# Block stages: three passes over the inner tiles instead of three products per tile

## The chip, the cores and the metric

The kernel runs on one core of a Trainium2 chip. The metric is the device time of one execution in microseconds (us). The engines are TensorE (PE in the profile; PEld is its loading of weights), VectorE (DVE), ScalarE (ACT), GpSimd (POOL) and SyncE (SP), which here only issues DMAs.

## The reference, cut to what matters

A first block (two recurrent branches and a mixture of experts) is followed by a second one with two layers. Each layer of the second block ends in a chain of dense steps, and it is this chain that the change touches:

```python
x = x + g1 * yx                       # yx = o @ w_out, o from attention or from the gated recurrence
hx2 = rms_norm_2(x, norm2_g[layer]) * (1.0 + sc2) + sh2
x = x + g2 * conv_glu(hx2, ffn_w_up[layer], ffn_conv_w[layer], ffn_conv_b[layer], ffn_w_down[layer])

def conv_glu(h, w_up, conv_w, conv_b, w_down):
    gate, val = jnp.split(h @ w_up, 2, axis=-1)
    return (jax.nn.silu(dwconv3(gate, conv_w, conv_b)) * val) @ w_down
```

There are 512 tokens and 256 context tokens, 1024 model columns, and 2816 columns inside the feed forward part. Layer 0 works on all 768 tokens, and behind its feed forward part comes the norm and the input projection of layer 1; layer 1 works on 512 tokens.

## The kernel before

`ffn_chain` is one stage for one such chain. It is called twice: as f0 for layer 0 (768 tokens, with a "tail", the input projection of layer 1) and as f1 for layer 1 (512 tokens, no tail, the last stage of the program). All activations stay in on-chip memory, transposed, as tiles of 128 model columns by all tokens.

Every float32 product is made of three: each operand is split into a high part of reduced precision (`w_hi`, `x_hi`, made by a cast on ScalarE) and a low part (`w_lo`, `x_lo`, the difference, made on VectorE), and TensorE adds up high by high, high by low and low by high in PSUM.

The weights come in units of one 128-column output tile each. `WeightUnits` has three slots: SyncE loads unit u when unit u - 3 was used, ScalarE casts it (`hi_part`, L2195, semaphore `hi_done`), VectorE makes the low part (`lo_part`, L2200, semaphore `ready`), and `products` (L2211) runs a unit's matmuls. f0 has 8 units of 8 inner tiles for `w_out`, 44 of 8 for the up projection (gate and value in turn), 16 of 11 for the down projection (two per output tile), and 32 of 8 for the tail. In f0 each inner tile and part has two matmuls, for the 512 tokens and the 256 context tokens; in f1 it has one.

Before, `products` waits for both parts of the unit's weights, and then goes through the inner tiles k; for each k it runs all three products:

```python
        pe.wait_ge(self.ready, u + 1)
        for k in range(tiles):
            if x_ready is not None:
                pe.wait_ge(x_ready, k0 + k + 1)
            for part, xs in ((w_hi, x_hi), (w_hi, x_lo), (w_lo, x_hi)):
```

`x_ready` is given only for the first unit after the activations change, since they are made tile by tile while that unit runs. These places are four in f0 and three in f1: the start of the stage (the input is loaded in four DMAs of two tiles, ScalarE casts each at L2367, VectorE makes the low tiles at L2440), the first up unit (behind a norm: per tile VectorE scales at L2426, ScalarE shifts at L2358 and casts at L2361, VectorE makes the low tile at L2433), the first down units (ScalarE casts 22 tiles at L2391, VectorE makes their low parts at L2480), and in f0 the first tail unit (behind a norm again). The semaphores for high tiles existed before (`in_hi`, `shifted`, `ff_hi`); VectorE waits on them.

Each engine's program is straight code in the order as written. `x_hi`, `x_lo` and the high part of the 22 feed forward tiles share one buffer, which the profile calls f_a_lo (also where it is the high part); the low part of the feed forward tiles is f_ff_lo.

Of the kernel before, what the change touches and what calls it, by code (L numbers as in the profile page):

```python
# [49 lines left out]
class SplitOperands:  # L50
# [77 lines left out]
    def products(self, pe, bank, s, col, span, spans):  # L128

        cols = slice(col * P, (col + 1) * P)  # L130
        for k in range(self.k_tiles):
            if col == 0 and k % (self.k_tiles // self.CHUNKS) == 0:
                pe.wait_ge(self.x_ready, k * self.CHUNKS // self.k_tiles + 1)
            hi, lo = self.w_hi[s][:, k, cols], self.w_lo[s][:, k, cols]
            for part, xs in ((hi, self.x_hi), (hi, self.x_lo), (lo, self.x_hi)):
                for h in range(spans):
                    last = pe.matmul(bank[:, h, 0:span], part, xs[:, k, h * span:(h + 1) * span],  # L137
                                     start=(k == 0 and xs is self.x_hi and part is hi), stop=(k == self.k_tiles - 1 and part is lo))
        return last


def dense_split(nc, name, w, x_v, out_v, k_tiles, tokens, groups, width):
# [5 lines left out]
    with Stage(nc) as ctx:  # L148
# [8 lines left out]
        with nc.Block() as block:  # L157
# [5 lines left out]
            @block.tensor  # L163
            def _(pe):
                pe.sem_inc(acc_ready, cols)

                def products(g, s, i, more):
                    pe.wait_ge(ops.w_ready, g + 1)
                    for c in range(cols):
                        pe.wait_ge(evacuated[c % 2], g * half + (c // 2 + 1))  # L170
                        ops.products(pe, acc[c % 2], s, c, span, spans).then_inc(acc_ready, 1)
                each_group(pe, groups, products)
# [187 lines left out]
LAT, CTX = 512, 256  # L360
# [9 lines left out]
def rwkv(nc, pt, loras, params, edges, consts, ya):  # L370
# [6 lines left out]
    with Stage(nc) as ctx:  # L377
# [85 lines left out]
        with nc.Block() as block:  # L463
# [352 lines left out]
            def _(pe):  # L816
# [189 lines left out]
                for i in range(TILES):  # L1006
                    prepare(i)
                    for k in range(8):
                        if k == 2:
                            pe.wait_ge(ops_ready, 2 * i + 1)  # L1010
                        transposes(i, k)
                    pe.wait_ge(ops_ready, 2 * i + 2)
                    for c in range(6):
                        products(i, c)
                        transposes(i, 8 + c)
                        if i and c == 1:
                            bonus_gate(i - 1)
                    for n in range(2):
                        left(i, n)
                    for u in range(2):  # L1020
                        values(i, u)
                    left(i, 2)
                    values(i, 2)
                    value_outputs(i)
                    left(i, 3)
                    for n in range(3, N_UNITS):
                        if n + 1 < N_UNITS:
                            left(i, n + 1)
                        right(i, n)
                    solve(i, 0)  # L1030
                    for c in range(6):
                        if c < 5:
                            solve(i, c + 1)
                        apply(i, c)
# [358 lines left out]
KD = D // P  # L1393
# [777 lines left out]
class WeightUnits:  # L2171
# [28 lines left out]
            dve.tensor_tensor(self.view(self.w_lo, u), self.view(self.w_raw, u), self.view(self.w_hi, u).bitcast(F32), ALU.subtract).then_inc(self.ready, 1)  # L2200

    def products(self, pe, u, acc, x_hi, x_lo, spans, k0=0, first=True, last=True, x_ready=None):
        pe.wait_ge(self.ready, u + 1)
        w_hi, w_lo = self.view(self.w_hi, u), self.view(self.w_lo, u)
        tiles = w_hi.shape[1]
        for k in range(tiles):
            if x_ready is not None:
                pe.wait_ge(x_ready, k0 + k + 1)
            for part, xs in ((w_hi, x_hi), (w_hi, x_lo), (w_lo, x_hi)):
                for a, b in spans:  # L2210
                    op = pe.matmul(acc[:, a:b], part[:, k], xs[:, k0 + k, a:b], start=(first and k == 0 and part is w_hi and xs is x_hi),  # L2211
                                   stop=(last and k == tiles - 1 and part is w_lo))
        op.then_inc(self.used, 1)
        return op


def ffn_chain(nc, name, tokens, o_in, w_o, x_in, up, conv, down, x_out, gate_mod, first, second, tail=()):


    spans = [(0, LAT)] + ([(LAT, TOK)] if tokens > LAT else [])  # L2220
# [7 lines left out]
    U0, D0 = KD, KD + 2 * FT  # L2228
    H0 = D0 + 2 * KD
# [5 lines left out]
    with Stage(nc) as ctx:  # L2235
# [3 lines left out]
        def sem(n):  # L2239
            return ctx.sem(f"{name}_{n}")  # L2240

        w = WeightUnits(ctx, name, units, 3, SPLIT * P)
# [12 lines left out]
        acc = [ctx.enter_context(nc.psum_tensor(f"{name}_acc{b}", [P, 2 * BANK], F32)) for b in range(3)]  # L2255
# [4 lines left out]
        in_hi, in_ready = sem("in_hi"), sem("in_ready")  # L2260
# [6 lines left out]
        shifted = [sem("h_shifted"), sem("t_shifted")]  # L2267
        h_ready = [sem("h_ready"), sem("t_ready")]
        pads, gate_ready, value_ready, gate_done, conv_done, sig_done, value_done = (sem(n) for n in (
            "pads", "gate_ready", "value_ready", "gate_done", "conv_done", "sig_done", "value_done"))  # L2270
        ff_hi, ff_ready = sem("ff_hi"), sem("ff_ready")
# [4 lines left out]
        x_hi, x_lo, o_raw = a_buf[:, 0:KD], a_buf[:, KD:2 * KD], a_raw[:, KD:2 * KD]  # L2276
# [3 lines left out]
        with nc.Block() as block:  # L2280
            @block.sync
            def _(sp):
                w.load(sp, 0)
                for c in range(4):
                    k = slice(2 * c, 2 * c + 2)
                    sp.dma_start(o_raw[:, k], o_in[:, k, 0:tokens]).then_inc(in_loaded[c], 16)  # L2286
                    if c == 0:
                        w.load(sp, 1)
                w.load(sp, 2)
                sp.dma_start(x[:], x_in[:, 0:tokens].rearrange("(k p) t -> p k t", p=P)).then_inc(loaded, 16)  # L2290
                for n, m in enumerate((gate_mod, (tail and second["mod"]) or first["mod"])):
                    sp.dma_start(mod[:, n].rearrange("p k s -> p (k s)"), m[0]).then_inc(loaded, 16)  # L2292
                    sp.dma_start(bias[:, n], m[1]).then_inc(loaded, 16)  # L2293
                sp.dma_start(gains[:, 0], first["gain"]).then_inc(loaded, 16)
                sp.dma_start(cpar[:], conv).then_inc(loaded, 16)
                sp.dma_start(ones[:], first["ones"]).then_inc(loaded, 16)
                if to_tail:
                    sp.dma_start(gains[:, 1], second["gain"]).then_inc(loaded, 16)
                for u in range(3, len(units)):
                    w.load(sp, u)  # L2300

            @block.tensor
            def _(pe):
                def column_sums(p):
                    pe.wait_ge(sq_added[p], KD - 2)
                    for a, b in spans:
                        pe.matmul(sums[:, a:b], ones[:], sq[0][:, a:b], start=True, stop=False)
                    pe.wait_ge(sq_done[p], KD)
                    for a, b in spans:
                        last = pe.matmul(sums[:, a:b], ones[:], sq[1][:, a:b], start=False, stop=True)  # L2310
                    last.then_inc(sums_done[p], 1)

                for c in range(KD):
                    if c >= 3:
                        pe.wait_ge(x_upd[0], c - 2)
                    w.products(pe, c, acc[c % 3], x_hi, x_lo, spans, x_ready=in_ready if c == 0 else None)
                column_sums(0)
                for t in range(FT):
                    n = U0 + 2 * t
                    if t >= 2:  # L2320
                        pe.wait_ge(value_done, t - 1)
                    w.products(pe, n, acc[n % 3], x_hi, x_lo, spans, x_ready=h_ready[0] if t == 0 else None)
                    if t >= 1:
                        pe.wait_ge(gate_done, t)
                    w.products(pe, n + 1, acc[(n + 1) % 3], x_hi, x_lo, spans)
                for c in range(KD):
                    if c >= 3:
                        pe.wait_ge(x_upd[1], c - 2)
                    n = D0 + c
                    for half in range(2):  # L2330
                        w.products(pe, D0 + 2 * c + half, acc[n % 3], a_buf, ff_lo, spans, k0=half * SPLIT, first=half == 0, last=half == 1,
                                   x_ready=ff_ready if c == 0 else None)
                if to_tail:
                    column_sums(1)
                for j, (dst, g, toks) in enumerate(outs):
                    if j >= 3:
                        pe.wait_ge(t_out[(j - 3) % 2], (j - 3) // 2 + 1)
                    w.products(pe, H0 + j, acc[(D0 + KD + j) % 3], x_hi, x_lo, spans if toks > LAT else spans[0:1], x_ready=h_ready[1] if j == 0 else None)

            @block.scalar  # L2340
            def _(act):
# [908 lines left out]
```

## Time and profile before

| | us |
|---|---|
| median of 3 runs (6059.99 to 6069.65) | 6060.88 |
| the profiled execution | 6060.24 |
| its span, first to last instruction | 6058.6 |
| TensorE busy | 4644.3 (77%) |
| VectorE busy | 2772.8 (46%) |
| ScalarE busy | 1519.5 (25%) |
| matmuls of L2211 on high weights and f_a_lo | 4048, 1028.1 busy |

The trace is one execution, and times in it count from the span's start. f0 lies at about 4313 to 5275 us, f1 at 5617 to the end. "Busy" of a matmul is a modelled duration that overlaps the next one; the pace of a stream is read from the starts. The granted TensorE clock is given as a share of 2.4 GHz: 1.00 is 2.4 GHz and 0.50 is 1.2 GHz.

### The profile page before, as it was taken

What the parts mean: (1) busy time and instruction counts of PE and PEld (TensorE: products, weight loads), DVE (VectorE), ACT (ScalarE), POOL (GpSimd) and SP (SyncE); (2) the same over time, 40 slices, a digit from 0 to 9 for tenths busy, and PEclk for the clock granted to TensorE, in tenths of its full rate; (3) what the DMA queues carried; (4) which work ended last, traced back from release to release, by engine and by line L of the source; (5) the groups of instructions that cost most, each with busy time, mean ns of one, the idle gap of its engine ahead of it and who ended that gap; (6) DMA issues with size and microseconds to landing.
All of it is one profiled execution on the core that took longest, in us unless ns stands there. A gap on an engine that the chain in (4) does not pass through costs nothing. (4 is left out here: it accounts for less than half of the span.)

```text
span 6058.6 us, 90639 instructions
## 1 busy us (share of the span) xinstructions
PE 4644.3 (77%) x38154; PEld 3616.5 (60%) x38154; DVE 2772.8 (46%) x4332; ACT 1519.5 (25%) x2328; POOL 448.1 (7%) x452
## 2 busy tenths in 40 slices
PE   4998968888875444574578867667899999888899
PEld 3997856777763333352322226444678878677687
DVE  2784256676656666322200012445444422267453
ACT  2111123222322222212100002233332221265322
POOL 0000010110002222100000000111100000000000
PEclk7999979999986666787789988667899999999999
DMA  5775210000000000233299933100211213401332
GB/s 214 271 262 206 104 47 12 12 16 20 6 16 31 30 30 14 112 134 138 77 421 422 422 155 121 41 15 15 84 56 63 70 63 110 146 32 44 111 96 96
DMA packets 174783, 656.20 MB, mean 108 GB/s; under 512 B 23584, under 2 KB 37024, under 8 KB 145760
## 3 DMA queue, kind: packets, MB, share of 16 engines
q1 hardware_dynamic: 159264, 582.96, 26.1%
q0 software_dynamic: 15168, 68.16, 3.0%
q8 instruction: 269, 4.41, 0.3%
q14 instruction: 82, 0.67, 0.0%
HBM read 554.44 MB, written 96.62 MB: 107 GB/s over the span
## 5 line engine op out<-in xcount | busy, mean ns | idle before, releaser
L2211 PE MATMUL f_acc<-f_a_lo,f_w_hi 128*128 128x512 f32 x4048 | 1028.1, 356 | 62.4 <-DVE f_a_lo L2440 27.3
L2211 PEld LDWEIGHTS f_acc<-f_a_lo,f_w_hi 128*128 128x128 f32 x4048 | 667.0, 190 | 183.1 <-issue 39.6
L2211 PE MATMUL f_acc<-f_a_lo,f_w_lo 128*128 128x512 f32 x2288 | 685.8, 355 | 0.0
L2200 DVE TENSOR_TENSOR f_w_lo<-f_w_raw,f_w_hi 128x1024 fp32r<-128x1024 f32 (+1 forms) x176 | 228.4, 1298 | 534.1 <-ACT f_w_hi L2195 534.1
L2211 PEld LDWEIGHTS f_acc<-f_a_lo,f_w_lo 128*128 128x128 f32 x2288 | 378.1, 190 | 62.3
L2195 ACT CAST f_w_hi<-f_w_raw 128x1024 fp32r<-128x1024 f32 (+1 forms) x176 | 194.5, 1105 | 608.6 <-DMA f_w_raw<-in_ffn_w_up 215.4
L655 DVE COPY_PREDICATED rw_work<-rw_mask_x,rw_big 128x512 f32<-128x512 uint8 x288 | 238.8, 881 | 155.2 <-PE rw_big L946 149.6
L1855 PE MATMUL ex_big<-ex_w,ex_xe_now 128*64 128x512 f32 x1024 | 239.4, 622 | 78.6 <-DMA ex_w<-in_exp_w 78.6
L946 PE MATMUL rw_big<-rw_work,rw_halves 128*64 128x64 f32 x4608 | 259.6, 222 | 0.8 <-issue 0.7
L257 DVE CUSTOM_DVE_ANT_0 in_both_mod_junk<-in_both_mod_rows,in_both_mod_vec 128x1024 f32<-128x1024 f32 x192 | 236.8, 1233 | 26.0 <-issue 1.6
L137 PE MATMUL in_both_acc<-in_both_x_hi,in_both_w_hi 128*128 128x384 f32 x704 | 185.7, 345 | 67.8 <-DVE in_both_x_lo L118 40.5
L943 PE MATMUL rw_big<-rw_halves,rw_work 128*64 128x64 f32 x3840 | 232.9, 222 | 1.1 <-issue 1.0
L946 PEld LDWEIGHTS rw_big<-rw_work,rw_halves 128*64 128x64 f32 x4608 | 225.4, 138 | 1.5 <-issue 1.4
L1901 DVE TENSOR_TENSOR ex_sg<-ex_sg,ex_big 128x512 f32<-128x512 f32 x16 | 11.0, 688 | 458.1 <-ACT ex_sg L1889 458.1
L1855 PEld LDWEIGHTS ex_big<-ex_w,ex_xe_now 128*64 128x64 f32 x1024 | 74.4, 143 | 241.9 <-issue 141.0
L943 PEld LDWEIGHTS rw_big<-rw_halves,rw_work 128*64 128x64 f32 x3840 | 200.3, 138 | 1.6 <-issue 1.5
L926 PE MATMUL rw_big<-rw_work,rw_mg 128*64 128x64 f32 x5376 | 189.0, 222 | 10.3 <-DVE rw_mg L651 7.0
L137 PE MATMUL in_both_acc<-in_both_x_lo,in_both_w_hi 128*128 128x384 f32 x704 | 183.4, 342 | 0.0
L137 PE MATMUL in_both_acc<-in_both_x_hi,in_both_w_lo 128*128 128x384 f32 x704 | 182.9, 341 | 0.0
L926 PEld LDWEIGHTS rw_big<-rw_work,rw_mg 128*64 128x64 f32 x5376 | 173.1, 137 | 14.5 <-DVE rw_mg L651 8.9
L137 PEld LDWEIGHTS in_both_acc<-in_both_x_hi,in_both_w_hi 128*128 128x128 f32 x704 | 131.1, 194 | 71.0 <-issue 39.3
L1334 PE MATMUL ss_big<-ss_xbc 128*128 128x128 f32 x32 | 8.3, 441 | 209.4 <-DVEq L1182 209.4
(519 smaller groups left out, 9024.9 us busy)
## 6 DMA issues: line engine op xcount, KB each, us to landing
ex_w<-in_exp_w SPq DMA_DIRECT2D x192, 1024.0 KB, 17.5
in_both_mod_rows<-in_ada_rows SPq DMA_DIRECT2D x128, 512.0 KB, 4.8
f_w_raw<-in_ffn_w_up SPq DMA_DIRECT2D x88, 512.0 KB, 3.5
f_w_raw<-in_ffn_w_down SPq DMA_DIRECT2D x32, 704.0 KB, 4.0
in_both_w_raw<-in_w_in_both SPq DMA_DIRECT2D x10, 2048.0 KB, 9.4
in_lat_w_raw<-in_w_in_lat SPq DMA_DIRECT2D x9, 2048.0 KB, 8.0
pt<-in_both_stage POOLq DMA_DIRECT2D x11, 1536.0 KB, 7.3
f_w_raw<-in_hgrn_w_both SPq DMA_DIRECT2D x24, 512.0 KB, 3.5
```

The source lines that it names most:

```text
L137: last = pe.matmul(bank[:, h, 0:span], part, xs[:, k, h * span:(h + 1) * span], start=(k == 0 and xs is self.x_hi and part is hi), stop=(k ...
L257: last = dve.tensor_tensor_reduce(self.junk[:], self.slot[b % self.SLOTS][:], self.vec[:, v], 1.0, 0.0, ALU.mult, ALU.add, self.res[:, b, ...
L655: return dve.copy_predicated(out, mask, data)
L926: last = pe.matmul(in_halves(T_BANK[n % 2], q, m, lv), mg[:, slot(BA, d, c, h), m[0]:m[1]], work_ap(xs_at + ((d * 6 + c) * 2 + h) * CH + ( ...
L943: pe.matmul(in_halves(X_BANK[n % 2], q, m, lv), work_ap(x_at + m[0], [[1, 64]]), t1_ap(n % 2, t_at + (d << lv), split(lv)), start=True, st ...
L946: last = pe.matmul(in_halves(XT_BANK[n % 2], q, m, lv), t1_ap(n % 2, t_at + m[0], [[1, 64]]), work_ap(x_at + ((1 - d) << lv), split(lv)), ...
L1334: last = pe.matmul(big[:, inter_bank, c * CH:(c + 1) * CH], token_tile(xbc[:, 4], c), token_tile(xbc[:, 5], c), start=True, stop=True)
L1855: last = pe.matmul(big[64 * half:64 * half + 64, 2 * par + m, :], xe_now[par][:, kh * KH + k], w13[kh][:, m, half, k], start=(kh == 0 and ...
L1901: dve.tensor_tensor(sg[:], sg[:], big[:, 2 * par, :], ALU.mult)
L2195: act.copy(self.view(self.w_hi, u), self.view(self.w_raw, u)).then_inc(self.hi_done, 1)
L2200: dve.tensor_tensor(self.view(self.w_lo, u), self.view(self.w_raw, u), self.view(self.w_hi, u).bitcast(F32), ALU.subtract).then_inc(self.r ...
L2211: op = pe.matmul(acc[:, a:b], part[:, k], xs[:, k0 + k, a:b], start=(first and k == 0 and part is w_hi and xs is x_hi), stop=(last and k = ...
```

## The change

`products` turns its loops around: the kind of product is the outer loop and the inner tile the inner one. All tiles high by high, then all high by low, then all low by high. The unit now begins with a wait for the high weights, and the wait for the low weights stands before the third pass. `x_ready` becomes a triple: the semaphore for high tiles, how many tiles one count of it stands for, and the semaphore for low tiles. The first pass waits for the high tile, the second for the low one. Callers hand over the semaphores that exist already. Nothing else changes; line numbers behind the edit move by 4 or 5.

```diff
     def products(self, pe, u, acc, x_hi, x_lo, spans, k0=0, first=True, last=True, x_ready=None):
-        pe.wait_ge(self.ready, u + 1)
+
+        pe.wait_ge(self.hi_done, u + 1)
         w_hi, w_lo = self.view(self.w_hi, u), self.view(self.w_lo, u)
         tiles = w_hi.shape[1]
-        for k in range(tiles):
-            if x_ready is not None:
-                pe.wait_ge(x_ready, k0 + k + 1)
-            for part, xs in ((w_hi, x_hi), (w_hi, x_lo), (w_lo, x_hi)):
+        for n, (part, xs) in enumerate(((w_hi, x_hi), (w_hi, x_lo), (w_lo, x_hi))):
+            if n == 2:
+                pe.wait_ge(self.ready, u + 1)
+            for k in range(tiles):
+                if x_ready is not None and n == 0:
+                    pe.wait_ge(x_ready[0], (k0 + k) // x_ready[1] + 1)
+                if x_ready is not None and n == 1:
+                    pe.wait_ge(x_ready[2], k0 + k + 1)
                 for a, b in spans:
-                    op = pe.matmul(acc[:, a:b], part[:, k], xs[:, k0 + k, a:b], start=(first and k == 0 and part is w_hi and xs is x_hi),
-                                   stop=(last and k == tiles - 1 and part is w_lo))
+                    op = pe.matmul(acc[:, a:b], part[:, k], xs[:, k0 + k, a:b], start=(first and n == 0 and k == 0), stop=(last and n == 2 and k == tiles - 1))
...
-                    w.products(pe, c, acc[c % 3], x_hi, x_lo, spans, x_ready=in_ready if c == 0 else None)
+                    w.products(pe, c, acc[c % 3], x_hi, x_lo, spans, x_ready=(in_hi, 2, in_ready) if c == 0 else None)
...
-                    w.products(pe, n, acc[n % 3], x_hi, x_lo, spans, x_ready=h_ready[0] if t == 0 else None)
+                    w.products(pe, n, acc[n % 3], x_hi, x_lo, spans, x_ready=(shifted[0], 1, h_ready[0]) if t == 0 else None)
...
-                                   x_ready=ff_ready if c == 0 else None)
+                                   x_ready=(ff_hi, 1, ff_ready) if c == 0 else None)
...
-                    w.products(pe, H0 + j, acc[(D0 + KD + j) % 3], x_hi, x_lo, spans if toks > LAT else spans[0:1], x_ready=h_ready[1] if j == 0 else None)
+                    w.products(pe, H0 + j, acc[(D0 + KD + j) % 3], x_hi, x_lo, spans if toks > LAT else spans[0:1], x_ready=(shifted[1], 1, h_ready[1]) if j == 0 else None)
```

TensorE, first up unit of f1, behind the sums of the norm (`f1_a_lo` is here `x_hi` or `x_lo`, `f1_w_hi2` the high and `f1_w2_lo` the low weights of slot 2). Before:

```order
L2310 MATMUL f1_sums<-f1_conved,f1_ones 128x512
L2211 MATMUL f1_acc2<-f1_a_lo,f1_w_hi2 128x512 x2
L2211 MATMUL f1_acc2<-f1_a_lo,f1_w2_lo 128x512
L2211 MATMUL f1_acc2<-f1_a_lo,f1_w_hi2 128x512 x2
L2211 MATMUL f1_acc2<-f1_a_lo,f1_w2_lo 128x512
```

And now:

```order
L2314 MATMUL f1_sums<-f1_conved,f1_ones 128x512
L2216 MATMUL f1_acc2<-f1_a_lo,f1_w_hi2 128x512 x16
L2216 MATMUL f1_acc2<-f1_a_lo,f1_w2_lo 128x512 x8
L2216 MATMUL f1_acc0<-f1_a_lo,f1_w_hi0 128x512 x16
L2216 MATMUL f1_acc0<-f1_a_lo,f1_w0_lo 128x512 x8
```

The x16 are 8 matmuls with `x_hi` and 8 with `x_lo`: what was interleaved tile by tile is now in three runs, inside each unit; the units keep their order.

TensorE, first down unit of f1, where high and low tiles are in different buffers (`f1_a_lo` is the high part). Before:

```order
L2211 MATMUL f1_acc1<-f1_a_lo,f1_w_hi1 128x512
L2211 MATMUL f1_acc1<-f1_ff_lo,f1_w_hi1 128x512
L2211 MATMUL f1_acc1<-f1_a_lo,f1_w1_lo 128x512
L2211 MATMUL f1_acc1<-f1_a_lo,f1_w_hi1 128x512
L2211 MATMUL f1_acc1<-f1_ff_lo,f1_w_hi1 128x512
L2211 MATMUL f1_acc1<-f1_a_lo,f1_w1_lo 128x512
```

And now:

```order
L2216 MATMUL f1_acc1<-f1_a_lo,f1_w_hi1 128x512 x11
L2216 MATMUL f1_acc1<-f1_ff_lo,f1_w_hi1 128x512 x11
L2216 MATMUL f1_acc1<-f1_a_lo,f1_w1_lo 128x512 x11
L2216 MATMUL f1_acc1<-f1_a_lo,f1_w_hi2 128x512 x11
L2216 MATMUL f1_acc1<-f1_ff_lo,f1_w_hi2 128x512 x11
```

All eleven low tiles are now read behind all eleven high ones, and the second unit of the output tile begins with its own eleven high ones.

## Rows read from the trace of the kernel before

**Rows 1.** Stage f0: window, length, busy us (count) per engine, clock, DMA
```profile
4313.00:5275.00 962.00, 922.46 (x5104) 797.94 (x5104) 346.15 (x378) 244.09 (x291) 17.41 (x24) 0.98 0.26 86
```

**Rows 2.** TensorE's waits, f0, then f1: total us, times, longest
```profile
PE f_acc L2211 <- DVE f_a_lo L2433: 19.3, 11, 6.2
...
PE f_acc L2211 <- DVE f_w_lo L2200: 1.7, 1, 1.7
...
PE f_acc L2211 <- DVE f_a_lo L2433: 6.3, 4, 4.6
...
PE f_acc L2211 <- DVE f_w_lo L2200: 2.0, 1, 2.0
```

**Rows 3.** Windows of f0; the clock is the number behind POOL's
```profile
4404.10:4410.30 6.20, 6.18 (x18) 4.75 (x18) 5.48 (x6) 6.01 (x10) 0.00 (x0) 0.50 0.00 0
4410.40:4417.90 7.50, 5.06 (x23) 3.68 (x23) 5.75 (x6) 7.25 (x11) 0.00 (x0) 0.95 0.00 0
...
4421.00:4778.60 357.60, 357.60 (x2064) 315.19 (x2063) 156.76 (x174) 82.48 (x110) 0.00 (x0) 1.00 0.21 65
...
4977.10:4980.30 3.20, 3.20 (x9) 2.60 (x10) 2.74 (x4) 3.08 (x6) 0.00 (x0) 0.50 0.00 0
```

**Rows 4.** Timeline, f1, down projection: start, us, engine, line, op, out<-in
```profile
5941.18 0.39 PE L2211 MATMUL f_acc<-f_a_lo,f_w_hi 128*128 128x512 f32 x1
5941.41 0.39 PE L2211 MATMUL f_acc<-f_ff_lo,f_w_hi 128*128 128x512 f32 x1
5941.63 0.39 PE L2211 MATMUL f_acc<-f_a_lo,f_w_lo 128*128 128x512 f32 x1
```

**Rows 5.** Timeline, f0, norm before the up projection: last cast, second unit's start
```profile
4417.09 0.83 ACT L2361 CAST f_a_lo<-f_conved 128x768 fp32r<-128x768 f32 x1
...
4420.83 0.86 PE L2211 MATMUL f_acc<-f_a_lo,f_w_hi 128*128 128x512 f32 x4
```

**Rows 6.** Timeline, f0, norm before the tail: last cast, second unit's start
```profile
4990.09 0.84 ACT L2361 CAST f_a_lo<-f_conved 128x768 fp32r<-128x768 f32 x1
...
4993.11 0.85 PE L2211 MATMUL f_acc<-f_a_lo,f_w_hi 128*128 128x512 f32 x4
```

**Rows 7.** Timeline, f1, norm: last cast, second unit's start
```profile
5690.13 0.62 ACT L2361 CAST f_a_lo<-f_conved 128x512 fp32r<-128x512 f32 x1
...
5692.34 0.63 PE L2211 MATMUL f_acc<-f_a_lo,f_w_hi 128*128 128x512 f32 x2
```

**Rows 8.** Timeline, start of f0: last cast of the input, unit 2
```profile
4326.39 1.48 ACT L2367 CAST f_a_lo<-f_a_raw 128x1536 fp32r<-128x1536 f32 x1 [0.47 <-DMA f_a_raw<-att]
...
4341.62 0.96 PE L2211 MATMUL f_acc<-f_a_lo,f_w_hi 128*128 128x512 f32 x4 [1.70 <-DVE f_w_lo L2200]
```

**Rows 9.** Timeline, start of f1: last cast, unit 2's weights, unit 2
```profile
5627.90 1.05 ACT L2367 CAST f_a_lo<-f_a_raw 128x1024 fp32r<-128x1024 f32 x1 [0.30 <-DMA f_a_raw<-hg]
...
5637.29 1.05 ACT L2195 CAST f_w_hi<-f_w_raw 128x1024 fp32r<-128x1024 f32 x1 [7.39 <-DVEq L2452]
...
5639.65 0.74 PE L2211 MATMUL f_acc<-f_a_lo,f_w_hi 128*128 128x512 f32 x2 [1.96 <-DVE f_w_lo L2200]
```

**Rows 10.** Timeline, f0, down projection: casts, low parts, third unit's start
```profile
4778.79 16.26 ACT L2391 CAST f_a_lo<-f_ff_raw 128x768 fp32r<-128x768 f32 x22 [2.19 <-PE f_acc L2211]
...
4779.80 19.19 DVE L2480 TENSOR_TENSOR f_ff_lo<-f_ff_raw,f_a_lo 128x768 fp32r<-128x768 f32 x22
...
4805.42 0.51 PE L2211 MATMUL f_acc<-f_a_lo,f_w_hi 128*128 128x512 f32 x2
```

**Rows 11.** Timeline, f1, down projection: casts, low parts, first unit, third unit's start
```profile
5926.87 11.54 ACT L2391 CAST f_a_lo<-f_ff_raw 128x512 fp32r<-128x512 f32 x22
...
5929.32 13.33 DVE L2480 TENSOR_TENSOR f_ff_lo<-f_ff_raw,f_a_lo 128x512 fp32r<-128x512 f32 x22
5930.15 0.76 PE L2211 MATMUL f_acc<-f_a_lo,f_w_hi 128*128 128x512 f32 x1 [3.69 <-DVE f_ff_lo L2480]
...
5947.98 0.39 PE L2211 MATMUL f_acc<-f_a_lo,f_w_hi 128*128 128x512 f32 x1
```

## The prediction

> **What bounds the kernel now.** The change touches one kind of stage, the fused block stage ffn_chain, which runs twice: f0 (768 tokens, a matmul of 512 and one of 256 columns for each weight tile) and f1 (512 tokens, one matmul). I first cut the span by stage. f0 takes 962 us and TensorE is busy in 922 of them [rows 1], so what TensorE does there sets the time, and what the others do counts only where TensorE stands. Then I asked what it stands for: besides the wait for the first data, it waits 19.3 and 6.3 us for the low halves of the normalized activations (L2433) and 1.7 and 2.0 us for low halves of weights [rows 2]. These are the waits that the change could shorten. Last I read the timeline around each place where `x_ready` is passed, because only there do the new waits bite. Everywhere else the operands were there long before: from 4421.0 to 4778.6 TensorE is busy 357.6 of 357.6 us, with 2064 matmuls [rows 3], 173 ns each, 0.3465 us for a pair of 512 and 256. In f1 a matmul of 512 follows the last by 0.227 us [rows 4].
>
> **The steady stream: nothing.** Number and size of the matmuls are the same (6,864), only their order changes. Before, two of three follow a matmul on another weight tile and one reuses w_hi; the spacing is 0.23 us from f_a_lo to f_ff_lo on the same w_hi and 0.22 to 0.23 after a change of weights [rows 4]. So a new order has no price per matmul. The new wait on hi_done instead of ready opens a unit one subtraction earlier, which gives nothing while TensorE is still in the unit before. All of the effect is in the seven first units.
>
> **What a first unit costs.** Before, k-tile by k-tile: as soon as tile k is there, TensorE does all three products on it, so when the last tile arrives only its own three are left. After, only the high by high product can run while the tiles trickle in; when the last high tile is there, its own high by high pair and the two other passes over 8 tiles remain: 1 + 16 = 17 pairs. The low parts are no longer waited for (the last one comes 1 us after its high part and is needed at the end of the second pass). The price is 17 pairs minus what was left before.
>
> The norm before the up projections of f0: the last high part ends at 4417.09 + 0.83 = 4417.92; 17 x 0.3465 = 5.9 gives 4423.8, where the next unit started at 4420.83 before [rows 5]: +3.0 us.
> The norm before the tail of f0: 4990.93 + 5.9 = 4996.8 against 4993.11 [rows 6]: +3.7.
> The norm of f1: 5690.75 + 17 x 0.227 = 5694.6 against 5692.34 [rows 7]: +2.3.
> The start of f0: high parts come two tiles at a time, the last pair at 4326.39 + 1.48 = 4327.87. 18 pairs, then unit 1 with 24 pairs: 4327.87 + 42 x 0.3465 = 4342.4. Before, unit 2 started at 4341.62, after 1.7 us for its w_lo [rows 8]; that wait is covered now. Net +0.8.
> The start of f1: 5628.95 + 42 x 0.227 = 5638.5; the high weights of unit 2 are there at 5637.29 + 1.05 = 5638.34, and before it started at 5639.65 [rows 9]: -1.2. Here the separate wait pays.
> The down projection of f0: 22 casts in 16.26 us, 0.739 each, so tile 10, the last of the first unit, is high at 4778.79 + 11 x 0.739 = 4786.9. Left are 1 + 11 + 11 pairs and 33 of the second unit: 56 x 0.3465 = 19.4, end 4806.3 against 4805.42 before: +0.9. The low tiles come every 0.87 us from 4780.7 and the eleventh at 4789.4, before its pair at 4790.8 [rows 10], so they don't hold it.
> The down projection of f1: the casts are done with tile 10 at 5926.87 + 11 x 0.5245 = 5932.6, but low tile 10 only at 5929.32 + 11 x 0.606 = 5936.0, which ends the second pass at 5936.2; 11 + 33 matmuls then give 5946.2 against 5947.98 before [rows 11]: -1.8. Before, TensorE stood 3.7 us for the first low tile and then crept at 1.2 GHz; now its first high tile is there at 5927.4 and the unit starts 2.7 us earlier.
> Sum at full clock: 3.0 + 3.7 + 2.3 + 0.8 - 1.2 + 0.9 - 1.8 = +7.7 us.
>
> **The clock.** These places follow idle time, and there the granted clock is 0.50, the 1.2 GHz level: after the norm in f0 for 6.2 us of busy work, before the tail for 3.2 us [rows 3]. Each microsecond of half clock in a full stream costs half a microsecond. Before, that creep was hidden: the tiles came every 2.1 us and three half-clock pairs on one tile take 2.07 us (18 matmuls, 9 pairs, in 6.2 us [rows 3]), so TensorE kept up, and when the last tile came the clock was mostly back (0.95 from 4410.4 to 4417.9, at 5.06 busy us of 7.5) [rows 3]. After, TensorE does one pair per tile during the norm, 0.7 us at half clock in 2.1 us. I expect it to stay at 1.2 GHz through the chain, and to creep only when the 17 pairs come, all of it on the path. For the three norms I take a half-clock stretch of 4.7 us, midway between 3.2 and 6.2, so +2.35 each; for the four other places, where TensorE is busier while tiles arrive, half of that, +1.2 each. That is 7.05 + 4.8 = 11.85, in all +19.5 us. If the clock is full in all seven, the sum is +7.7; with 6.2 us at half clock in all seven, 7 x 3.1 = 21.7, it is +29.4.
> The Trainium skill, page "TensorE: Matmul & The Clock Gate", section "Loop structure matters more than you think", says that matmuls with a wait between each leave the array at the low clock, while a dense stream over the k-tiles keeps it up. By that rule the first pass is the bad form, and the sum is the one with the clock in it, +19.5. The row from 4410.4 to 4417.9 agrees only in part: with TensorE busy for 5.06 of 7.5 us the clock was up for most of it; by this row alone the sum would lie nearer +7.7.
>
> **Where the loss could hide.** Behind each place TensorE works without a gap to the next norm (the row of 357.6 us is the stretch behind the first), the weights are loaded and split ahead of it, and the vector and scalar engines wait for it. So a delay of a first unit moves everything behind it. Casts and subtractions of the activations run in the same order with the same waits as before and gain nothing.
>
> **The rivals.** (1) The clock doesn't fall, or returns as the passes get dense: +7.7 plus a few, below 12. For it: the 0.95 row. Against: one pair per tile is a third of the work that held it there. Time 6060.9 + 8 = 6069; chance 0.17. The same page, section "What's actually happening", has it that the default state is throttled and activity releases it; with the pair of each tile counted as enough activity the result would be this one.
> (2) Faster: the pace of the stream. At 0.227 us a matmul of 512 takes 14 ns more than 512 columns at 2.4 GHz (213 ns). If runs of matmuls on the same moving buffer shed part of that, 6,864 matmuls pay it back: 19.5 / 6.864 = 2.8 ns each brings the sum to nothing, and from 4.6 ns each it is faster by more than 12 us; with 7 ns, half of the 14, 48 - 19.5 = 28.5 us faster, 6032. Against: the equal spacing in rows 4 across all three kinds of neighbours. Chance 0.03. The same mechanism the other way (2 ns more each, +14) is in the upper end, 0.03.
> (3) The change doesn't do what it says, or the delays are absorbed: if TensorE had slack behind a first unit, only the earlier starts would count, at most 1.7 + 2.0 us [rows 2], and the time is 6060.9 - 4 to 6060.9. Against: the row without a gap. Chance 0.04.
>
> **How the numbers follow.** The profiled execution took 6060.24 us with a span of 6058.6; +19.5 makes 6079.7, and on the median of 6060.88 it is 6080.4. That is the forecast, chance 0.73 with all the amounts of half clock that give more than 12. The range goes from 6067, just under the case at full clock, to 6091, which holds all but the last of the extreme at half clock; what is left out is some 0.15. A measurement of this kernel can tell 0.2%, 12.1 us, from no change. Slower by more: 0.73 + 0.03 = 0.76. Within: 0.17 + 0.04 = 0.21. Faster: 0.03.
>
> **What would show it.** In the profile after: the unit behind each norm ends about 17 pairs behind the last high cast; in that stretch the granted clock is 0.50 for 3 to 6 us; TensorE waits for the scalar engine's casts (L2361 and L2391 of now) instead of the vector engine's low parts; no wait for w_lo at unit 2; and the stretch of 2064 matmuls takes 357.6 us again. The prediction is wrong if the clock is at 1.00 in those stretches (then +8), if that stretch changes its length (then the pace), or if f0 grows by less than its first units do.

## The result

| | before | after |
|---|---|---|
| median, us | 6063.33 (7 runs, 6056.63 to 6069.65) | 6087.62 (7 runs, 6077.59 to 6104.80) |
| profiled execution, us | 6060.24 | 6081.76 |
| its span, us | 6058.6 | 6080.1 |
| mean granted clock | 0.866 | 0.865 |

The ratio is 1.0042, with a 95% interval of 1.0028 to 1.0055: the changed kernel is slower by some 25 us (17 to 33). The prediction was 6080.4 us, 6067 to 6091.

The profile of the changed kernel shows the new wait. TensorE's waits from the start of f0 to the end (engine, its line, what it waited for, us in total, times, longest):

```profile
PE f_acc L2216 <- ACT f_a_lo L2365: 34.9, 24, 5.2
PE f_acc L2216 <- ACT f_a_lo L2371: 29.9, 6, 13.2
...
PE f_acc L2216 <- ACT f_a_lo L2395: 2.2, 2, 1.2
```

The 19.3 and 6.3 us for the low half of the normalized tiles [rows 2] are gone, and so are the 1.7 and 2.0 us for low weights. In their place stand 34.9 us for ScalarE's cast of the same tiles (L2365): TensorE now has one pair of matmuls to do for each tile and then stands until the next. The second row is the wait for the first data of each stage, which was there before as well (27.3 us, then for the low halves); the third is the down projections.

What is put off comes behind the last tile. The timeline of the norm before the up projections of f0 answers to [rows 5] (start, duration, engine, line, operation, count, idle time before):

```profile
4409.49 0.83 ACT L2365 CAST f_a_lo<-f_conved 128x768 fp32r<-128x768 f32 x1
...
4410.38 5.03 PE L2216 MATMUL f_acc<-f_a_lo,f_w_hi 128*128 128x512 f32 x18 [1.16 <-ACT f_a_lo L2365]
...
4415.24 2.98 PE L2216 MATMUL f_acc<-f_a_lo,f_w_lo 128*128 128x512 f32 x16
...
4418.06 0.76 PE L2216 MATMUL f_acc<-f_a_lo,f_w_hi 128*128 128x512 f32 x3
```

The last cast ends at 4410.32. Then come 18 matmuls (the last tile's pair and the whole pass of the low activations), 16 on the low weights, and only at 4418.06 the next unit: 7.7 us behind the cast, where it was 2.9 before. The first 18 take 4.9 us, 0.54 a pair; the 16 behind them 2.8, 0.353 a pair. The windows show the clock of both (bounds, length, busy us and count of PE, PEld, DVE, ACT, POOL, then the granted clock):

```profile
4410.40:4415.00 4.60, 4.60 (x17) 3.97 (x18) 2.85 (x3) 1.05 (x1) 0.00 (x0) 0.62 0.00 0
5001.40:5005.90 4.50, 4.50 (x18) 3.88 (x19) 2.10 (x2) 0.83 (x1) 0.00 (x0) 0.67 0.00 0
5708.90:5712.80 3.90, 3.90 (x9) 3.11 (x10) 2.35 (x3) 1.05 (x1) 0.00 (x0) 0.50 0.01 2
4403.00:4410.30 7.30, 3.02 (x6) 1.51 (x6) 5.60 (x6) 7.07 (x10) 0.00 (x0) 0.50 0.00 0
...
4418.20:4782.70 364.50, 364.50 (x2065) 315.97 (x2063) 155.64 (x173) 82.55 (x110) 0.00 (x0) 1.00 0.20 64
```

The first three are the stretches behind the three norms: TensorE is busy throughout and granted 0.62, 0.67 and 0.50. The fourth is the norm itself, where TensorE is busy 3.0 of 7.3 us, at 0.50, the 1.2 GHz level. The last is the stretch up to the down projection, which answers to the 357.6 us of [rows 3]. It holds one matmul more and takes 364.5 us. That was not expected, and it is followed up below.

Every place can be measured in the traces as one distance. A: start of f0 (VectorE's first instruction of the stage, L2435) to unit 2. B, D, F: the three norms, end of the last cast to the next unit's first matmul. C, G: first feed forward cast to the third down unit, in f0 and f1. E: start of f1 to unit 2. In us, from one profile each (the last six rows are the kernels of experiments 3 to 8, in that order):

| | A | B | C | D | E | F | G | sum |
|---|---|---|---|---|---|---|---|---|
| before | 28.35 | 2.91 | 26.62 | 2.19 | 22.02 | 1.60 | 21.11 | 104.8 |
| before, again | 28.13 | 2.22 | 25.07 | 2.86 | 21.89 | 1.59 | 21.19 | 102.9 |
| after | 31.35 | 7.73 | 28.12 | 7.52 | 22.66 | 6.57 | 19.58 | 123.5 |
| after, again | 31.32 | 7.48 | 28.12 | 7.41 | 22.69 | 6.84 | 19.56 | 123.4 |
| first units by tile | 26.73 | 1.85 | 25.07 | 1.84 | 20.76 | 1.36 | 19.64 | 97.3 |
| first units in passes | 31.19 | 7.44 | 28.12 | 8.87 | 22.33 | 6.74 | 19.55 | 124.2 |
| first units two, then low | 28.68 | 5.61 | 26.41 | 5.48 | 22.18 | 3.99 | 19.77 | 112.1 |
| passes with filler | 31.48 | 6.16 | 28.11 | 6.15 | 23.09 | 4.04 | 19.53 | 118.6 |
| first units split | 26.88 | 1.49 | 24.73 | 1.51 | 21.66 | 1.12 | 19.30 | 96.7 |
| split, filler ahead | 27.24 | 1.50 | 24.73 | 1.51 | 21.12 | 1.12 | 17.82 | 95.0 |

After less before is +18.7 us for the first pair of profiles and +19.6 for the means of two; predicted was +19.5. Single places of before differ between its two profiles by up to 1.6 us, and the clock goes with it: B took 2.91 us with the clock at 0.54 from 4417.10 to 4420.80, and 2.22 us in the second profile, at 1.00; C took 26.62 us with 0.66 in its first 5 us, and 25.07 at 1.00. The rest of the 21.5 us between the two profiled spans is worked out in the section on the prediction.

### The profile page after: what moved, and what is told of

The parts are those of the page before. It is cut to its first block and busy times, and to the rows that moved or that the text cites. A ratio compares the mean times of both kernels' runs of the same rounds, so it can differ in the third digit from the quotient of the medians.

```text
span 6080.1 us, 90639 instructions
## 1 busy us (share of the span) xinstructions
PE 4662.5 (77%) x38154; PEld 3618.8 (60%) x38154; DVE 2772.4 (46%) x4332; ACT 1521.3 (25%) x2328; POOL 449.1 (7%) x452
## 5 line engine op out<-in xcount | busy, mean ns | idle before, releaser
L2216 PE MATMUL f_acc<-f_a_lo,f_w_hi 128*128 128x512 f32 x4048 | 840.3, 363 | 67.9 <-ACT f_a_lo L2365 34.9
L2216 PE MATMUL f_acc<-f_a_lo,f_w_lo 128*128 128x512 f32 x2288 | 469.3, 355 | 0.0
```

## The experiments

In the experiments `products` goes through a list `steps` of pairs (n, k), with n = 0 for high by high, 1 for high weights by low activations and 2 for low weights by high activations. It waits for `hi_done` ahead of the first step, for `ready` ahead of the first n = 2, and for each tile's high or low half when it is first read; `x_ready` is given only at the seven places. Only this list is changed unless more is said.

**1 and 2. The same two kernels once more.** One profile each, unchanged, to see what a trace repeats.

> The kernel before once more, for its profile. Question: the spacing of a pair of 512 and 256 column matmuls in f0, which was 346.7 ns in the stretches behind the norms and 353.3 ns in one stretch of 51 us in the first profile. Theory 'order': in tile by tile order the stream runs at 346.7 ns behind each norm again, since the spacing is a property of the order (one place at most at 353.3). Rival 'chance': each stretch falls on one of the two spacings after a stall whatever the order, and another profile of the same kernel shows another mixture, up to four stretches at 353.3 (f0 up to 14 us longer).

> The changed kernel once more, for its profile. Its first profile showed 353.3 ns in all stretches of f0. Theory 'order': again 353.3 everywhere. Rival 'chance': some stretches at 346.7 ns, f0 up to 14 us shorter. Both expect the first units' delays as in the first profile (unit behind the norm ends about 30.6 and 32.1 us behind the start of the column sums, against 25.8 and 25.1 before).

Measured: 6063.03 and 6077.17 us. Both theories, that the pace goes with the order, failed, and the rival 'chance' held, as the windows below show. The sums of the places repeat within 1.9 and 0.1 us; a single place repeats within 0.3 us in after and within 0.7 in before, but for C with 1.55. Spans do not repeat as well: of 19 runs of before beside these, the fastest took 6052.70 and the slowest 6079.81. And the stream's pace had changed places. The window of 300 us in the up projections, the kernel before, first profile:

```profile
4450.00:4750.00 300.00, 300.00 (x1732) 264.56 (x1732) 128.43 (x144) 67.03 (x91) 0.00 (x0) 1.00 0.20 64
```

The same kernel again:

```profile
4450.00:4750.00 300.00, 300.00 (x1700) 260.04 (x1699) 125.80 (x142) 65.75 (x88) 0.00 (x0) 1.00 0.19 62
```

The changed kernel, first profile:

```profile
4450.00:4750.00 300.00, 300.00 (x1700) 260.17 (x1699) 127.22 (x143) 65.68 (x89) 0.00 (x0) 1.00 0.20 62
```

And again:

```profile
4450.00:4750.00 300.00, 300.00 (x1732) 264.51 (x1731) 128.51 (x145) 67.03 (x91) 0.00 (x0) 1.00 0.20 64
```

1732 or 1700 matmuls, 0.3464 or 0.3529 us a pair, all at full clock and with no gap: each order shows both. So the 364.5 us of after are not the order's doing. Over the twelve profiles with 512 and 256 in turn, the slower pace holds in 14 of 24 stretches of f0 by tile and in 17 of 24 in passes, too few to tell a difference.

**3 and 4. The change in two halves.** The kernel of 3 has the old order in the first units and passes everywhere else, that of 4 the reverse.

```diff
+        steps = [(n, k) for k in range(tiles) for n in range(3)] if x_ready is not None else [(n, k) for n in range(3) for k in range(tiles)]
...
+        steps = [(n, k) for n in range(3) for k in range(tiles)] if x_ready is not None else [(n, k) for k in range(tiles) for n in range(3)]
```

> Only the seven first units (those with x_ready) go tile by tile again, with the waits kept apart; all other units run in three passes. Theory 'first units and order': the delays of the first units, +20 us in the profile, go and become about -3 (each starts a subtraction earlier), but the stream stays at 353.3 ns per pair, +14: 11 us over before, about 6074. Rival 'first units alone': the passes cost nothing in the stream, and the time is 3 us under before, about 6060. Rival 'entry': the spacing is set by the unit in which the stream becomes dense, so tile by tile there gives 346.7 ns behind it.

> The reverse: the seven first units in three passes, all others tile by tile (as before, but for a wait on the high weights ahead of the unit and one on the low weights at its third product). Theory 'first units and order': +20 us of delays stay, and the stream is back at 346.7 ns: about 6083 (before at 6063). Rival 'chance' or 'entry': also 353.3 ns in the stretches behind the first units, +34, about 6097.

Measured: with passes in all but the first units, 6062.70 us, ratio 1.0004 (0.9991 to 1.0018), -5 to +11 us. With passes in the first units alone, 6085.37 us, ratio 1.0031 (1.0015 to 1.0047), +19 us (9 to 28). The seven places are those of after (124.2), but for D, which took 1.35 us more; the clock behind its last cast was 0.50 for 6.2 us, against 3.1 in after. The loss lies in the first units, as the theory and its rival 'first units alone' both say. What the theory added, a slower stream wherever passes run, did not hold. Kernel 3 was to take 11 us more than before and its median is 1 us lower (its interval ends just at 11), and kernel 4, by tile, was to run at 346.7 ns, but its up and down units ran at 353.3 and the other two stretches at 346.7. 'Entry' fails too: kernel 3 is by tile where the stream becomes dense, and ran at 353.3. 'Chance' fits the paces, though not the +34 us that it was given for kernel 4.
One more miss: the places of kernel 3 are 5.7 to 7.5 us shorter than before's, since its units start on the high parts, but its median is not lower. Its profile had the slow pace, 353.3 ns, in all four stretches of f0; from ten runs with a spread of 25 us a gain of 6 us can't be told.

**5. How the cost follows the work left over.** In the first units the low weights' pass alone is put last:

```diff
+        steps = [(n, k) for k in range(tiles) for n in range(2)] + [(2, k) for k in range(tiles)] if x_ready is not None else [(n, k) for n in range(3) for k in range(tiles)]
```

> As the changed kernel, but the seven first units run high by high and high by low together per tile and only low by high as a pass of its own. Read at the norms: time from the end of the last high cast to the start of the next unit. It was 2.9, 2.2 and 1.6 us before (the three norms) and 7.7, 7.5 and 6.5 with three passes. Theory 'what is left behind': the last low tile comes about 1.0 us (0.75 in f1) after the cast, then 1 + 8 pairs of 0.35 are left: 4.1, 4.1 and 2.8 us plus up to 2 us of half clock. Rival 'clock or waits, not the count': stays near 7.5.

Measured: 5.6, 5.5 and 4.0 us behind the three norms, against 4.1, 4.1 and 2.8 (plus up to 2 for the clock). It lies between the old order (2.2 to 2.9 in f0 and 1.6 in f1, with three pairs left) and three passes (7.6, 7.5, 6.7, with 17), as the count of pairs left demands; the rival, near 7.5, is out. The timeline behind the norm before the up projections:

```profile
4411.92 2.00 PE L2220 MATMUL f_acc<-f_a_lo,f_w_hi 128*128 128x512 f32 x4 [0.16 <-ACT f_a_lo L2369]
...
4413.72 3.92 PE L2220 MATMUL f_acc<-f_a_lo,f_w_lo 128*128 128x512 f32 x16
...
4417.48 5.71 PE L2220 MATMUL f_acc<-f_a_lo,f_w_hi 128*128 128x512 f32 x32
```

The last tile's four matmuls take 1.8 us, 0.9 a pair with a wait for the low half in between, and the 16 behind them 3.76 instead of 2.8: TensorE is still at the lower clock for part of the dense work (0.50 from 4411.90 to 4415.80). The one run took 6063.17 us, too little to read from its total.

**6. The clock's share.** Three passes as in after, but between the tiles of the first pass TensorE does five matmuls (three in f1) on weights that lie there already, into a buffer that nobody reads at that time. The output is as before; the fillers are extra work.

```diff
+            if each and n == 0 and k < tiles - 1:
+                for _ in range(each):
+                    pe.matmul(spare[:, 0:512], w_hi[:, 0], self.w_hi[u % self.slots][:, 0:512], start=True, stop=True)
```

> The changed kernel, with five (f1: three) extra matmuls of 512 columns into an unused accumulator after each tile of the first pass of the three units behind a norm, where TensorE waits for the next tile: work that is thrown away, to keep the granted clock up. Theory 'part of the delay is the half clock': from the last cast to the next unit 5.9, 5.9 and 3.9 us (17 pairs at full clock) instead of 7.7, 7.5 and 6.5, with a granted clock of 1.00 there. Rival 'no clock in it': unchanged.

Measured behind the three norms: 6.16, 6.15 and 4.04 us, where 17 pairs at full clock make 5.9, 5.9 and 3.9. The fillers do not hold the casts back: from the start of the last matmul ahead of the norm to the end of its last cast it took 25.5, 25.5 and 18.4 us, and 25.5, 27.1 and 18.4 in after. The windows of the stretch behind the norm, and of the norm with its fillers:

```profile
4441.60:4446.90 5.30, 5.30 (x30) 4.60 (x31) 2.80 (x3) 1.05 (x1) 0.00 (x0) 1.00 0.01 3
4426.70:4441.50 14.80, 13.57 (x49) 9.86 (x49) 12.22 (x13) 14.34 (x21) 0.00 (x0) 0.85 0.00 0
```

and the timeline:

```profile
4441.53 3.45 PE L2222 MATMUL f_acc<-f_a_lo,f_w_hi 128*128 128x512 f32 x18 [0.39 <-ACT f_a_lo L2374]
...
4444.82 2.98 PE L2222 MATMUL f_acc<-f_a_lo,f_w_lo 128*128 128x512 f32 x16
```

The same 18 matmuls that took 4.9 us in after take 3.3 here, at a clock of 1.00. So of the 7.7, 7.5 and 6.6 us behind the norms in after, 1.6, 1.4 and 2.5 are the clock's, and the rest is the work itself. That agrees with the clock in the trace of after: behind the last casts it stayed at 0.50 for 3.5, 3.1 and 5.5 us, and half of that is 1.8, 1.6 and 2.8. The places without a filler, A, C, E and G, stand where they stood in after (the largest difference is 0.4 us). The whole run took 6108.72 us; it had reached f0 some 20 us later than before's first profile, in code that is the same in both, so nothing is read from its total.

**7 and 8. Each tile's work in the order in which its halves come.** High by high, low weights by high activations, then the one that needs the low activations; in 8 with four or five spare matmuls ahead of the units at the start of the stage and the down projection (extra work, output as before).

```diff
+        steps = [(n, k) for k in range(tiles) for n in (0, 2, 1)] if x_ready is not None else [(n, k) for k in range(tiles) for n in range(3)]
```

> The order of before in all but the first units, which go tile by tile as high by high, low by high, high by low, with the waits apart (the two products that need only the high tile run while the low tile is made). Theory: last cast to next unit 1.3 to 2.0 us at the norms (before 2.9, 2.2, 1.6), unit 2 at the starts 1.3 us earlier than before, the down projection of f1 begins 2.7 us earlier: in all 6 to 9 us under before in the stage's first units, 0.1% of the time, which the runs can hardly show; the choice of spacing (346.7 or 353.3 ns) stays a matter of chance, plus or minus 7 us.

> The same with five thrown-away matmuls of 512 columns ahead of the very first unit of each stage and four ahead of the first down unit, in time in which TensorE waits. Theory: the half clock stretch behind the wait at the down projections (3.3 us in f0, 5.8 us in f1 before) goes, worth 1.6 and 2.9 us: 10 to 13 us under before. Rival: the wait is too short to let the clock fall once the first high tile is enough, so the filler adds nothing over the kernel without it.

Measured: 6061.45 us, ratio 0.9994 (0.9982 to 1.0006), and 6058.56 us, 0.9992 (0.9982 to 1.0003). The places add up to 96.7 and 95.0 us, 6 to 10 below before, and are the best of all orders: 1.5 us behind both norms of f0. In time the gain can't be told from none. The fillers ahead save 1.5 us at G, where 2.9 were expected, and nothing at A and C, where C was to give 1.6. The clock tells the two down projections apart. At G the kernel of 7 does two matmuls, waits 1.7 us for the first low tile and goes on at half clock; with the fillers ahead the same matmuls run at 1.00 (first the kernel of 7, then that of 8):

```profile
5925.40:5928.90 3.50, 3.20 (x8) 2.52 (x9) 3.50 (x7) 3.50 (x8) 0.00 (x0) 0.51 0.02 6
...
5939.50:5943.00 3.50, 3.30 (x15) 2.74 (x16) 3.50 (x7) 3.50 (x8) 0.00 (x0) 1.00 0.02 9
```

At C the clock of the kernel of 7 was 1.00 already, from 4769.80 to 4793.50, so there was nothing to gain: there the rival held.

**9 to 11. What the stream's order is worth.** First units as in 7. In 9 the rest goes by tile (the kernel of 7 again), in 10 in passes as in the change, in 11 by tile but with all matmuls of 512 columns of a unit ahead of all of 256:

```diff
+        if x_ready is None and len(spans) > 1:
+            pe.wait_ge(self.ready, u + 1)
+            for a, b in spans:
+                for i, (n, k) in enumerate(steps):
+                    part, xs = ((w_hi, x_hi), (w_hi, x_lo), (w_lo, x_hi))[n]
+                    op = pe.matmul(acc[:, a:b], part[:, k], xs[:, k0 + k, a:b], start=(first and i == 0), stop=(last and i == len(steps) - 1))
```

> The kernel first_split_by_tile once more, as the partner of the next one on the same chip. By its first units 7.2 us under before; the spacing in f0 by chance.

> The first units as in first_split_by_tile, all other units in three passes. It parts what the passes do in the steady stream from what they do in the first units. Theory 'chance': the spacing of 346.7 or 353.3 ns does not depend on the order, and the median is that of split_rest_tile within the spread, some 3 us. Rival 'the passes favour 353.3': up to 14 us over it, and 353.3 ns in all stretches of the profile.

> As split_rest_tile, but where a unit of f0 has two token spans, all its 24 (33) matmuls of 512 columns come first and then all of 256. Theory 'the mixture costs': matmuls of 512 among themselves follow at 226.7 ns as in f1, those of 256 at half of it, 113.3, so a pair takes 340.0 ns instead of 346.7 or 353.3, and the choice between these two goes: 2,100 pairs x 6.7 to 13.3 = 14 to 28 us less than split_rest_tile, and less spread. Rival 'weight loads': a matmul of 256 columns is too short to hide the load of its weights, and pairs take more than 353 ns: slower.

| | median, us | ratio to before | 95% |
|---|---|---|---|
| 9, by tile | 6062.11 | 0.9997 | 0.9984 to 1.0010 |
| 10, in passes | 6062.18 | 0.9998 | 0.9985 to 1.0011 |
| 11, by span | 6052.49 | 0.9982 | 0.9970 to 0.9994 |

9 and 10 are the cleanest look at the change's other half: the same first units (their places add up to 95.8 and 96.0 us), twelve runs each on one chip, medians 0.07 us apart. The means are 2.4 us apart (-4 to +9, an estimate from the spread of the runs), so passes in the stream cost nothing that can be measured. 11 is faster than before by 11 us (4 to 18), and than 9, which has the same first units, by 8 us in the mean (2 to 14, estimated the same way). The expected 340 ns a pair was not reached:

```profile
4502.33 0.63 PE L2212 MATMUL f_acc<-f_a_lo,f_w_hi 128*128 128x512 f32 x2
...
4507.80 0.40 PE L2212 MATMUL f_acc<-f_a_lo,f_w_hi 128*128 128x256 f32 x2
...
4510.67 0.63 PE L2212 MATMUL f_acc<-f_a_lo,f_w_hi 128*128 128x512 f32 x2
```

From 4502.33 to 4507.80 there are 24 matmuls of 512 (0.228 us each) and to 4510.67 24 of 256 (0.120): 347.5 ns a pair. That is no faster than the quicker pace of the alternating order, but no stretch ran at its slower one. The rival, over 353 ns, is out.

**12. The fastest once more.** The kernel of 11, unchanged.

> The same kernel as split_span_outer once more. If its gain (0.18% under before, 0.06 to 0.30) is its own: a pair near 347.5 ns in every stretch of the profile again, and 0.1 to 0.25% under before. If it was the luck of the spacing: a stretch at 353 ns or more, and a ratio that can't be told from 1.

Measured: 6059.36 us against 6073.65, ratio 0.9978 (0.9968 to 0.9989). A pair took 347.5 ns again (347.3 in the down projection). Both comparisons have their whole interval below 1: this version beats the kernel before by 0.2%. Part of that is its first units, whose places are 6 to 10 us shorter in experiments 7 and 8. It was never run beside the changed kernel; by the two ratios it would beat it by 0.6%.

## Why the prediction was right, and where it was not

**What bounds the kernel, and that nothing absorbs a delay:** right. The seven places grew by 18.7 to 19.6 us and the kernel by 25 (17 to 33); rival 3 is out. Nor did anything behind a place give time back: in f1, the 233.7 us from the second up unit to the last and the 104.5 us from the third down unit to the last are the same before and after, within 0.1 us.

**The first units:** right, as a mechanism and nearly in size. Experiments 3 and 4 put the loss there by taking the change apart, and 5 shows that it goes with the work left over. Place by place, predicted (with its share of the clock) and measured in the first pair of profiles: A 2.0 and 3.0, B 5.3 and 4.8, C 2.1 and 1.5, D 6.1 and 5.3, E 0.0 and 0.6, F 4.6 and 5.0, G -0.6 and -1.5. The errors are up to 1 us and partly cancel. The norms measured 15.1 us of the 18.7 and were predicted at 16.0. At the down projection of f1 the separate wait pays, and the change gains there, as forecast.

**The clock:** right, its size too large. Predicted was 2.35 us for each norm, and experiment 6 took away 1.6, 1.4 and 2.5, together 5.5 instead of 7.05. For the four other places 1.2 us each was put down, and no run takes the clock away from all four. At A that was too small: in after the clock was 0.50 for 4.6 us behind the last cast of the input and in before not at all, 2.3 us, which with the 0.8 of the work makes some 3, as measured. Rival 1, a clock that stays up, would have left 5.9, 5.9 and 3.9 us behind the norms. The filled kernel shows these within 0.3 us and the changed one does not. The Trainium skill, page "TensorE: Matmul & The Clock Gate", section "Loop structure matters more than you think", holds that matmuls with a long wait for data between each run at the low clock and a dense stream over the k-tiles does not. This case agrees with the first half, though its waits are short, some 1.1 us each in f0: 0.50 for the first pass at 3.0 busy us of 7.3. With the second it agrees after a delay: the dense stretches just behind such passes were granted 0.50 to 0.67, and 1.00 only after that; where fillers close the gaps it was 0.85, then 1.00. The row of before that spoke against it, 0.95 at 5.06 busy of 7.5 us [rows 3], was no guide to the first pass, in which TensorE does less. It also missed that the clock fell again in that very trace, to 0.54 from 4417.10 to 4420.80.

**The steady stream:** the conclusion holds (experiments 3, 9 and 10: no gain and no price for the order that can be measured, so rival 2 is out), but the step under it failed. It took 0.3465 us a pair as a constant of the kernel, from one profile, and named a changed length of the 357.6 us stretch as proof of a new pace. That stretch did change, by 7 us, and the test would have given a false alarm: the pace is one of two values, and which one a stretch has differs between executions of the same kernel.

**From the places to the total.** After's profile was at the slow pace in the up, down and tail units, where before's had the quick one: 6.9, 3.1 and 3.7 us, in all 13.6, at 6.7 ns a pair. (The tail has 40 units, not 32 as the text ahead of the prediction has it, and pairs only in 24 of them; the other 16 have the 512 columns alone.) The stretch from the last down unit to the last cast of the norm behind it took 1.7 us more, which kernels of both orders show in some profiles. Against it, after reached f0 10.5 us earlier; the first cast of weights there is at 4306.08, in before at 4316.65, and no line before it had been changed. After:

```profile
4306.08 1.05 ACT L2195 CAST f_w_hi<-f_w_raw 128x1024 fp32r<-128x1024 f32 x1 [9.29 <-DMA f_w_raw<-in_attn_w_out]
```

Before:

```profile
4316.65 1.04 ACT L2195 CAST f_w_hi<-f_w_raw 128x1024 fp32r<-128x1024 f32 x1 [9.35 <-DMA f_w_raw<-in_attn_w_out]
```

18.7 + 13.6 + 1.7 - 10.5, less 1.7 that the gated recurrence between f0 and f1 took less, is 21.8, against 21.5 us between the spans. So the profiled pair came out within 2 us of the forecast partly by luck: two chance parts of over 10 us nearly cancelled. The ratio stands for 17 to 33 us, and the 19.5 that were forecast lie in it.

**Open:** why a stretch takes up the one pace or the other, and what makes the part before f0 end up to some 30 us apart between executions. Neither was tried. Open too is what the clock costs at C, E and G in the changed kernel.

## What to carry to other kernels

Where operands come tile by tile, do all that can be done with a tile when it comes, and first what needs only the half that comes first. Passes over all tiles put two thirds of the unit behind the last tile, and the pauses that they open before it can hold TensorE's clock down for just that work. The per-tile order with the products in the order of their halves was the shortest at the places here, 6 to 10 us under before, which the total times could not tell from none. Once all operands are there, the order of the three products cost nothing here. Judge a change of 0.2% by many runs, and compare the places in the trace that it touches, since the totals of two profiles differ by as much from chance.

## What the runs showed of the hardware

**Two paces for one stream.** In f0, where matmuls of 512 and 256 columns alternate, a pair takes 346.7 or 353.3 ns (2%). The pace changed only across a pause of TensorE and stayed for the whole stretch (42 of the 44 up units in a row, all at clock 1.00). Output projection, up, down and tail of one execution can differ: 353.3, 346.7, 346.7, 346.7 in before's first profile and 353.3, 353.3, 346.7, 353.3 in its second; after had 353.3 four times, then 353.3, 346.7, 353.3, 346.7. With the sizes in two groups per unit it was 347.3 to 347.5 in all eight stretches of two profiles (but for up to three units at a stretch's start), and in f1, where all have 512 columns, 226.7 ns each in every profile. The two paces together are worth up to 14 us of this kernel.

**Spare matmuls can pay.** Five per tile (three in f1) took 1.4 to 2.5 us off the places behind the norms; four ahead of the down projection took 1.5 us off in f1, where the clock had fallen to 0.51 without them, and nothing in f0, where it was 1.00 anyway; five ahead of the stage's start took nothing off in f0, and in f1 nothing beyond what that place varies (20.5 to 21.7 us without them).

**Short waits can hold the clock down.** In the first passes behind the norms in after, TensorE stood between its few matmuls on one tile and those on the next, for some 1.1 us each time in f0 and 0.6 to 0.8 us in f1. The granted clock was 0.50 throughout, and stayed there for 3.1 to 5.5 us of dense work behind the last tile.
